# First expert head in token halves, its top-k in three pieces, and output chunks inside the last block

## The reference, cut to what matters

```python
q = (xt @ wq).reshape(T, PEER_HEADS, 2, PEER_HALF)
sc = jnp.einsum('thpd,hpkd->thpk', q, subkeys)
vals, ids = lax.top_k(sc, PEER_TOPK)
cand = (vals[:, :, 0, :, None] + vals[:, :, 1, None, :]).reshape(T, PEER_HEADS, 256)
top, pos = lax.top_k(cand, PEER_TOPK)
idx = jnp.take_along_axis(cid, pos, axis=-1)
g = jax.nn.softmax(top, axis=-1)
...
a = jnp.einsum('chkd,cd->chk', u, xc)      # u: the rows of u_tab that idx picks
wgt = gc * jax.nn.gelu(a)
vv = jnp.take(v_tab, ic, axis=0)
return jnp.einsum('chk,chkd->cd', wgt, vv)
```

## Time and profile before

| what | us |
|---|---|
| median of 3 runs (lowest, highest) | 2702.19 (2696.27, 2703.08) |
| the profiled execution | 2704.44, its span 2702.6 |
| PE busy | 2581.7 (96%) |
| DVE busy | 1272.8 (47%) |
| POOL busy | 1100.0 (41%) |
| ACT busy | 666.4 (25%) |
| gate adds (L691), x384, first to last start | 1417.8 to 2172.4 |
| granted TensorE clock, mean over the span | 0.973 |

### The profile page before, as it was taken

How to read it: one execution, slowest core, us unless ns; L and a number is a source line. 1 busy time by engine, 2 the same in 40 slices (tenths; PEclk the granted TensorE clock), 3 DMA queues, 4 the chain that set the end, 5 groups by cost and what they waited for, 6 DMA issues and landing times.

```text
span 2702.6 us, 31994 instructions
## 1 busy us (share of the span) xinstructions
PE 2581.7 (96%) x11025; PEld 1382.8 (51%) x11025; DVE 1272.8 (47%) x2585; ACT 666.4 (25%) x1153; POOL 1100.0 (41%) x701
## 2 busy tenths in 40 slices
PE   6999899989999999879899999999999969999998
PEld 5776577734444444434345444444444435555555
DVE  2322354432223200564258798522222269888887
ACT  2212122310000001212121433322223323333332
POOL 0001111000000000000008888888888878888884
PEclk9999799999999999989999999999999979999999
DMA  6210100133453323274213666666666779999996
GB/s 158 75 48 0 44 13 9 63 124 125 134 177 125 95 64 90 67 259 176 78 63 49 132 152 152 152 152 153 152 153 153 166 267 390 369 365 366 367 364 238
DMA packets 420142, 424.27 MB, mean 157 GB/s; under 512 B 105945, under 2 KB 336345, under 8 KB 419937
## 3 DMA queue, kind: packets, MB, share of 16 engines
q1 hardware_dynamic: 342242, 355.88, 40.0%
q0 software_dynamic: 77824, 67.41, 11.6%
HBM read 362.15 MB, written 61.06 MB: 157 GB/s over the span
## 4 chain that ended last, share of the span: by engine, by line
PE 66%; POOL 24%; issue 5%; DVE 3%; ACT 1%; DMA 1%; SPq 0%; DVEq 0%; POOLq 0%; ACTq 0%
POOL dense_gates L691 24%; PE psum L1063 11%; PE psum L1119 8%; PE psum L797 7%; PE psum L1288 6%; PE psum L1289 6%; PE psum L1287 6%; PE psum L1092 6%; PE psum L967 1%; PE psum L801 1%; PE psum L983 1%; PE psum L1047 1%; PE psum L993 1%; PE psum L895 1%; PE psum L955 1%
## 5 line engine op out<-in xcount | busy, mean ns | idle before, releaser
L691 POOL DMA_INDIRECT dense_gates<-arena x384 | 639.5, 1665 | 435.8 <-DVE arena L2142 319.1
L1265 PE MATMUL psum<-arena 128*128 128x512 bf16 x1024 | 388.1, 379 | 0.0
L1266 PE MATMUL psum<-arena 128*128 128x512 bf16 x1024 | 388.1, 379 | 0.0
L1264 PE MATMUL psum<-arena 128*128 128x512 bf16 x1024 | 388.1, 379 | 0.0
L1287 PE MATMUL psum<-arena 128*128 128x384 bf16 x1024 | 333.0, 325 | 25.4 <-DVE arena L2181 25.4
L1288 PE MATMUL psum<-arena 128*128 128x384 bf16 x1024 | 337.0, 329 | 0.0
L1289 PE MATMUL psum<-arena 128*128 128x384 bf16 x1024 | 336.4, 328 | 0.0
L2147 DVE TENSOR_TENSOR arena<-arena 128x1024 bf16<-128x1024 f32 x128 | 158.4, 1238 | 364.7 <-ACT arena L1588 364.1
L1119 PE MATMUL psum<-arena 128*128 128x512 f32 x656 | 300.6, 614 | 20.2 <-ACT arena L1505 10.0
L1063 PE MATMUL psum<-arena 128*128 128x512 f32 x704 | 306.4, 596 | 5.0 <-DVE arena L1678 5.0
L684 POOL MEMSET arena<- 128x384 f32 x1 | 0.4, 417 | 624.3 <-DVE arena L1932 624.3
(11 more groups left out here) (315 smaller groups left out, 3041.5 us busy)
## 6 DMA issues: line engine op xcount, KB each, us to landing
arena<-in_uT SPq DMA_DIRECT2D x128, 512.0 KB, 4.5
arena<-in_v SPq DMA_DIRECT2D x128, 512.0 KB, 4.7
gelu_spill<-cst SPq DMA_DIRECT2D x128, 256.0 KB, 2.3
arena<-in_ada_w SPq DMA_DIRECT2D x12, 2048.0 KB, 13.0
dense_gates<-arena SPq DMA_DIRECT2D x4, 6144.0 KB, 39.8
arena<-gelu_spill SPq DMA_DIRECT2D x128, 192.0 KB, 4.7
arena<-dense_gates SPq DMA_DIRECT2D x128, 192.0 KB, 5.4
arena<-in_w_in SPq DMA_DIRECT2D x22, 1024.0 KB, 7.4
```

The costliest lines, as they stand in the source:

```text
L691: pool.indirect_dma_start(gate_cells, bass.IndirectOffsetOnAxis(ap=cell_of[:, n:n + 1], axis=0), gate_of[:, n:n + 1], None, compute_op=ALU ...
L1264: mm(psum[:, bank, :], hi[:, c, :], h2hi[:, c, :], start=c == 0, stop=False)
L1265: mm(psum[:, bank, :], hi[:, c, :], h2lo[:, c, :], start=False, stop=False)
L1266: last = mm(psum[:, bank, :], lo[:, c, :], h2hi[:, c, :], start=False, stop=c == DC - 1)
```

## The change

The stage of head 0 is rewritten. TensorE forms the products of its two query halves first for tokens 0 to 255, both interleaved chunk by chunk as the chunks of `u2` arrive, then half of the chunks of the first product for tokens 256 to 511, then the scores of tokens 0 to 255, then the rest; the scores of tokens 256 to 511 stand inside product 2. ScalarE's copies follow in halves. VectorE does head 0 in three pieces, t = 0, t = 1, and t = 2 to 3, each with its gates right behind its cells; GpSimd's adds of tile t wait for piece t. For later heads `slots_of(h)` stands right behind the cells of head `h`, that of head 1 behind the 20 parts that come before the up phase. In the last down block each output chunk's transpose follows its own matmuls, so `e_fin` counts transposes alone, and the wait for `row_sum` stands ahead of the block. The semaphore counts are renumbered.

```diff
 # TensorE
+            def half_query(u, half, bank, chunks):
+                lo = half * SH
+                for c in chunks:
+                    if half == 0:
+                        pe.wait_ge(S["shifted"], DC + c + 1)
+                    last = mm(psum[:, bank, 0:SH], slot_cols(F_WQ)[:, c, u * P:(u + 1) * P], u2[:, c, lo:lo + SH],
+                              start=c == 0, stop=c == DC - 1)
+                if c == DC - 1:
+                    last.then_inc(S["wq_done"], 1)
+            def half_scores(u, half):
+                pe.wait_ge(S["wq_taken"], 2 * half + u + 1)
+                if half:
+                    pe.wait_ge(S["sc_taken"], u + 1)
+                for t in (2 * half, 2 * half + 1):
+                    last = mm(psum[:, 2 + u, t * P:(t + 1) * P], qf[:, u, t * P:(t + 1) * P], subk[:, u, :], start=True, stop=True)
+                last.then_inc(S["sc_done"], 1)
...
+            for c in range(DC):
+                for u in range(2):
+                    half_query(u, 0, u, (c,))
+            half_query(0, 1, 6, range(0, 4))
+            for u in range(2):
+                half_scores(u, 0)
+            half_query(0, 1, 6, range(4, DC))
+            half_query(1, 1, 7, range(DC))
+            for u in range(2, 2 * PH):
...
+                if u >= 4:
+                    pe.wait_ge(S["wq_taken"], u + 1)
+                w, cols = slot_cols(n), slice(u % 4 * P, (u % 4 + 1) * P)
+                for c in range(DC):
+                    last = mm(psum[:, u % 2, :], w[:, c, cols], u2[:, c, :], start=c == 0, stop=c == DC - 1)
+                    if u == 2 and c == 1:
+                        for k in range(2):
+                            half_scores(k, 1)
+                last.then_inc(S["wq_done"], 1)
+                if u > 2:
                     scores(u - 1)
...
                     if stop:
-                        last.then_inc(S["e_fin"], 1)
+                        pe.transpose(psum[:, f, DEN:SEC], vsum[:, cols], const("ident")).then_inc(S["e_fin"], 1)
...
             for n in range(PK - 4, PK):
+                if n == PK - 1:
+                    pe.wait_ge(S["row_sum"], P)
                 down2(n, n % 4, False, n == PK - 1)
-            pe.wait_ge(S["row_sum"], P)
-            for f in range(DC):
-                pe.transpose(psum[:, f, DEN:SEC], vsum[:, f * P:(f + 1) * P], const("ident")).then_inc(S["e_fin"], 1)
 # ScalarE
+            for half in range(2):
+                for u in range(2):
+                    take_half(u, half)
+                if half:
+                    weigh_slots(0, 0, 1)
+                for u in range(2):
+                    take_half_scores(u, half)
+            for u in range(2, 2 * PH):
+                act.wait_ge(S["wq_done"], u + 3)
+                act.wait_ge(S["sc_done"], u + 1)
                 f_(qf[:, u % 2, :], psum[:, u % 2, :], ACT.Copy).then_inc(S["wq_taken"], 1)
-                if u:
+                if u > 2:
                     take_scores(u - 1)
-                if u == 4:
-                    weigh_slots(0, 0, 2)
-                elif u == 6:
+                if u == 2:
+                    weigh_slots(0, 1, 2)
+                elif u == 4:
                     weigh_slots(0, 2, SC)
-                elif u == 11:
+                elif u == 9:
                     weigh_slots(1)
 # VectorE
-                elif part == 7 and h > 1:
-                    slots_of(h - 1)
-                if part == 7 and h < PH:
+                elif part == 7:
...
                     dve.tensor_copy(by_slot(cell_of)[:, t0:t1, h], cell[:, t0:t1]).then_inc(S["tk_gate"], 1)
+                    if h > 1:
+                        slots_of(h)
...
-            for part in range(PARTS):
-                choose(0, part, 0, 2)
-            for part in range(2):
-                choose(0, part, 2, SC)
-            slots_of(0, 0, 2)
-            for part in range(2, PARTS):
-                choose(0, part, 2, SC)
-            slots_of(0, 2, SC)
+            for t0, t1 in ((0, 1), (1, 2), (2, SC)):
+                for part in range(PARTS):
+                    choose(0, part, t0, t1)
+                slots_of(0, t0, t1)
             for k in range(PARTS, AHEAD):
                 choose(*divmod(k, PARTS))
+            slots_of(1)
...
-                dve.wait_ge(S["e_fin"], DC + f + 1)
+                dve.wait_ge(S["e_fin"], f + 1)
 # GpSimd
-                    if h == 0 and t < 2:
-                        pool.wait_ge(S["tk_gate"], 2)
-                    else:
-                        pool.wait_ge(S["tk_gate"], 2 * (h + 2))
+                    pool.wait_ge(S["tk_gate"], 2 * (t + 1) if h == 0 else 2 * (h + 3))
```

More of the change, by code:

```diff
@@ L558, in _ @@
             for k in range(4):
-                reader, count = ("out2_done", 4 * (k + 1)) if k < 2 else ("wq_done", 4 * (k - 1))
+                reader, count = ("out2_done", 4 * (k + 1)) if k < 2 else ("wq_done", 4 * (k - 1) + 2)
                 fill(F_WQ + k, halves(F_WQ + k, wq[:, :, k * 512:(k + 1) * 512]), reader, count)
@@ L609, in _ @@
                     load_u(i * 4 + b + 5, b + 5)
-            sp.wait_ge(S["tk_gate"], 2 * (PH + 1))
+            sp.wait_ge(S["tk_gate"], 2 * (PH + 2))
             sp.wait_ge(S["tk_row"], PH)
@@ L1231, in _ @@
             pe.wait_ge(S["table_in"], 64)
+            SH = SEC // 2
+            def half_query(u, half, bank, chunks):
[14 more added lines that the diff above has]
+                last.then_inc(S["sc_done"], 1)
             def scores(u):
-                pe.wait_ge(S["wq_taken"], u + 1)
+                pe.wait_ge(S["wq_taken"], u + 3)
                 if u >= 4:
-                    pe.wait_ge(S["sc_taken"], u - 3)
+                    pe.wait_ge(S["sc_taken"], u - 1)
                 for t in range(SC):
@@ L1240, in scores @@
                 last.then_inc(S["sc_done"], 1)
-            for u in range(2 * PH):
+            pe.wait_ge(*fill_done(F_WQ))
+            for c in range(DC):
[7 more added lines that the diff above has]
+            for u in range(2, 2 * PH):
                 n = F_WQ + u // 4
@@ L1270, in _ @@
                 if b == 2:
-                    pe.wait_ge(S["sc_taken"], 2 * PH)
+                    pe.wait_ge(S["sc_taken"], 2 * PH + 2)
                 up(b, b, first=True)
@@ L1580, in take_scores @@
             def take_scores(u):
-                act.wait_ge(S["sc_done"], u + 1)
+                act.wait_ge(S["sc_done"], u + 3)
                 f_(scall[:, u].rearrange("p t k -> p (t k)"), psum[:, 2 + u % 4, :], ACT.Copy).then_inc(S["sc_taken"], 1)
@@ L1596, in weigh_slots @@
             def weigh_slots(h, t0=0, t1=SC):
-                act.wait_ge(S["tk_top"], h + 2 if t1 == SC else 1)
+                act.wait_ge(S["tk_top"], h + 3 if h else t0 + 1)
                 f_(ebest[:, t0:t1, h, :], ebest[:, t0:t1, h, :], ACT.Exp).then_inc(S["tk_exp"], 1)
@@ L1608, in w_high, with take_half, take_half_scores @@
                 f_(whl[b][0], wf[b], ACT.Copy).then_inc(S["w_hi"], 1)
[L1610 to L1613, removed]
+            SH = SEC // 2
+            def take_half(u, half):
+                act.wait_ge(S["wq_done"], 2 * half + u + 1)
+                f_(qf[:, u, half * SH:(half + 1) * SH], psum[:, 6 * half + u, 0:SH], ACT.Copy).then_inc(S["wq_taken"], 1)
+            def take_half_scores(u, half):
+                act.wait_ge(S["sc_done"], 2 * half + u + 1)
+                f_(scall[:, u, 2 * half:2 * half + 2].rearrange("p t k -> p (t k)"), psum[:, 2 + u, half * SH:(half + 1) * SH],
+                   ACT.Copy).then_inc(S["sc_taken"], 1)
+            for half in range(2):
[8 more added lines that the diff above has]
+                act.wait_ge(S["sc_done"], u + 1)
                 f_(qf[:, u % 2, :], psum[:, u % 2, :], ACT.Copy).then_inc(S["wq_taken"], 1)
-                if u:
+                if u > 2:
                     take_scores(u - 1)
-                if u == 4:
-                    weigh_slots(0, 0, 2)
-                elif u == 6:
+                if u == 2:
+                    weigh_slots(0, 1, 2)
+                elif u == 4:
                     weigh_slots(0, 2, SC)
-                elif u == 11:
+                elif u == 9:
                     weigh_slots(1)
@@ L2060, in choose @@
                 units = [(p, t) for p in range(2) for t in ts]
-                sco = scall[:, 2 * h:2 * h + 2] if h < PH else None
+                sco = scall[:, 2 * h:2 * h + 2]
                 pu = posu[:, t0:t1].rearrange("p a b -> p (a b)").bitcast(U32)
@@ L2064, in choose @@
                 if part == 0:
-                    dve.wait_ge(S["sc_taken"], 2 * h + 2)
+                    dve.wait_ge(S["sc_taken"], 2 if t1 <= 2 else 2 * h + 4)
                     for p, t in units:
```

4 lines of the change are left out of this document (1 added, 3 removed).

## The result

The changed kernel took 2684.24 us in the median of 5 runs (2676.57 to 2684.67), the kernel before in the same session 2698.28 us (2696.25 to 2703.08): ratio 0.9931, 95% interval 0.9916 to 0.9946, so 18.6 us less by the ratio. The two medians alone differ by 14.0 us; runs of one kernel scatter over as much as 8 us, so the median of five can fall near either end. The forecast was 2682.8 us within 2675 to 2691, and 19.4 us less.

A forecast was written before the change was run, and what follows sets the result against it. It took GpSimd's gapless gate adds to bound the seam, with TensorE the bound before and behind it, then a tail. Seam 16.0 plus tail 3.4 gives 19.4 us off the 2702.19 median: 2682.8 us, 8 in 10 range 2675 to 2691.

The forecast's parts named there:

- the seam: Between up and down phase: TensorE restarts at 2170.5 instead of 2186.53 us, a gain of 16.0 us, bounds 12.8 to 17.7.
- the tail: Last down block: VectorE's output chunks start while TensorE still multiplies and end 3.4 us earlier, 2.4 if transposes don't overlap.
- First gates: Head 0 in the query stage: gates ready at 1393.7, first add at 1394.7 us, a lead of 23.1 us.
- The extra cost of half products: TensorE's query stage: half products cost 0.5 us more in all, bounds 0 and 1.0.
- The stream stays gapless: GpSimd's gate adds: no add but the first waits for VectorE; last add at about 2148 us.
- The cap by the last store: SyncE's queue at the seam: gate loads follow the last activation store, so they start 13.3 us earlier, not 23.
- These are now over: At the seam: the four gathers of `v` no longer compete with the gate loads; fourth load landing taken as 3.7 us.
- The Trainium skill's sentence: DMA at the seam: 2.0 us fixed plus bytes over 436 GB/s, so four loads and the store take 4.3 us.
- (a): Rival, gate adds: the stream stays the bound if the lead is under 13.3 us; 2691 us at 8; chance 0.08.
- (b): Rival, down phase: it gives the seam's gain back as TensorE waits for transfers; 2699 us; chance 0.06.
- (c): Rival, gate adds: each takes longer, mean step 2.04 us eats the gain, 2.10 gives 2725.5 us; chance 0.03.
- (d): Rival, query stage: half products don't bring scores forward; 4 us of slack, time unchanged; chance within the forecast's 0.80.

The follow-up runs named there:

- whole_products: The changed kernel with head 0's queries and scores whole again, the three top-k pieces kept; ratio to before 0.9963.
- two_pieces: The changed kernel with head 0's top-k in two pieces (tokens 0 to 255, 256 to 511) instead of three; ratio to before 0.9939.
- early_loads: The changed kernel with SyncE's four first gate loads moved ahead of the last activation store; ratio to before 0.9916.
- add_late26: The changed kernel with GpSimd's first add held until all three pieces are ready; one run, 1332.30 us from query stage start, against 1331.91 before.
- early_rows_early: The changed kernel with the first four gathers of `v` ahead of the last 16 adds and gate loads ahead of the last activation store; ratio to before 0.9906.
- early_rows_later: The changed kernel with gate loads ahead of the last activation store and the first four gathers of `v` waiting for them to land; ratio to before 0.9921.
- add_late10: The changed kernel with GpSimd's first add held until piece 1 is ready too; ratio to before 0.9959.
- tail_only: The kernel before with only the last down block's edit, transposes following each chunk's matmuls; ratio to before 0.9993.

## Why the prediction was right

The mechanism came as forecast: an earlier first add, capped at the seam by the last activation store, and a separate tail. From the start of the query stage the profiled execution is 19.75 us shorter, with 15.6 at the seam (forecast 16.0) and 4.1 in the down phase (forecast 3.4, the tail). That the median of 2684.24 us lies within 1.5 us of the 2682.8 forecast is partly luck: the kernel before had a median of 2698.28 us beside it and not the 2702.19 that the sum started from.

- **First gates.** Forecast from the query stage's start: VectorE at 13.3, first add at 24.0. Measured 12.95 and 23.73. The one-tile piece took 1392.47 (the first instruction of its gates) - 1383.19 = 9.3 us against 9.1 from the line through the two longer pieces. `whole_products` and `two_pieces` show 13.0 and 6.0 us for the two parts.
- **The extra cost of half products** was put at 0.5 us; it is nothing. The last up block ends 790.48 us after the stage's start (2160.72 - 1370.24), before 790.41. The term was mis-sized: the 0.230 us came from the whole length of a row, in which the last matmul stands with its full duration of some 0.39 us. From start to start the 264-column matmuls take 0.224 us, which is 0.217 for 256 columns, and 0.216 was measured.
- **The stream stays gapless**: right, 116.7 us of issue as before. The forecast of its end, about 777 (2148), was 4 us early: the steps over the query stage are 1.92 us rather than the 1.87 that the prediction took from a window whose count includes adds cut by its edges, and the stream as a whole took 757.6 us instead of 754.6. The 4 us stayed hidden.
- **The cap by the last store**, 13.3 of 23 us: right. The loads leave 13.2 us earlier (791.59 against 804.76), and `early_loads` and `add_late26` show the two sides of it. The restart came 15.6 us earlier, forecast 16.0; the fourth load landed in 3.86 us where the row's minimum of 3.7 was taken, and from its landing to the first matmul it was 3.15 us instead of 2.78. "These are now over", said of the gathers, was only just true of the fourth load, issued at 2163.46 as the last gather landed at 2163.47, and not of the three loads before it.
- **The Trainium skill's sentence** (DMA: Bandwidth & Descriptors, Anatomy of one DMA), a fixed 2.0 us plus bytes, would by the prediction's estimate have put all four loads and the store at 4.3 us from the store's issue. Measured from the store's issue in the chain (2161.38) to the landing (2167.32) it was 5.9, so the row was the better guide for the four. That section of the Trainium skill gives its sum for transfers that GpSimd issues, and these are SyncE's. But the row's minimum of 3.7 us was not the uncrowded figure that the prediction called it: with the gathers out of the way the first of the four loads landed in 2.31 us (`early_rows_early`) and 2.47 us (`early_rows_later`), close to the 2.45 us that an estimate from the same section of the Trainium skill gives for 192 KB.
- **The tail**: forecast 3.4, measured 3.3 and 3.5.
- **The rivals.** (a) did not occur, and `add_late26` shows its regime. But its border was not where the prediction put it, at a lead of 13.3 us: a lead of 13.6 us (`add_late10`) or even 17.3 (`two_pieces`) already costs 7.4 and 3.6 us, since the gathers follow the adds and slow the loads. The sum was right because it had counted this contention once, in the landing of 6.97 against 3.7 us; what it missed is that the gathers use up the slack of 10 us. (b) was wrong for the changed kernel: from the restart to the start of the last transpose it took 507.84 us (2170.47 to 2678.31), where the prediction had set 508 as the sign of being wrong. It turned out true as soon as the gathers were moved behind the restart (519.06). (c) left a trace of 3 us in the stream: the mean step grew from 1.970 to 1.978 us, far from the 2.04 of the rival. Its comfort that the new early adds meet no worse neighbour rested on the 1.87; the first 96 steps of the stream before average 1.987 us, more than the whole. (d) did not occur: the first halves were copied from 1379.72 on.
- **A gain not forecast**: the down phase is 4.1 us shorter, the tail being 3.4 of it. The rest fits the clock after the restart, which the prediction left as it was: the granted clock is 0.50 over 2170.4 to 2174.5 us, before over 2186.5 to 2192.0, and 12 matmuls stand at the long spacing of 0.32 us instead of 17, an estimate of 5 x 0.16 = 0.8 us.

## What to carry to other kernels

When a long serial stream on one engine ends ahead of a barrier, its lead is worth only what lies up to the next thing in that barrier's queue; work out that cap before costing the lead. What stands right behind the stream in its own queue counts too: transfers issued there share the DMA engines with those that the barrier waits for, so slack must cover them as well. In both runs that moved the gathers from before the restart to behind it their time came back as a hole; moved into the up phase, where the DMA engines had room, they cost nothing in the trace.

## What the runs showed of the hardware

- Four loads of 192 KB, in the same place of the same queue: the fourth lands in 3.1 to 4.2 us when the four gathers (2 MB, GpSimd's queue) have landed when it is issued (within 0.15 us) or are not yet issued, in 6.4 to 9.3 us when the first of them leaves 1.2 to 3.2 us ahead of the loads. It was 6.4 to 7.2 us where the last activation store was some 6 us or more away (before, `tail_only`, `whole_products`, `add_late26`) and 8.2 to 9.3 us where it was near (`two_pieces`, `early_loads`, `add_late10`); that the store makes the difference was not tried alone.
- A product of two 256-column f32 halves takes TensorE the time of one of 512 columns: the 24 matmul rows from 1382.57 to 1387.76 are 0.216 us each, against 0.43.
- After 25.4 us of idle 17 matmuls ran at the long spacing of 0.32 us (before), after 9.7 us 12 (after), after 17.2 us 11 (`add_late10`), after 29.5 us 15 (`add_late26`): the length of the idle does not order them.
